# Reordering the time-mix projections of a two-layer block: k first, the low-rank products of decay and a between its passes

## The reference, cut to what matters

```python
xr, xw, xk, xv, xa, xg = (h + hh * mu[i] for i in range(6))
r = xr @ w_r
w = -jax.nn.softplus(-(w0 + jnp.tanh(xw @ w1) @ w2)) - 0.5   # w1: 1024 x 64
k = xk @ w_k
v = xv @ w_v
a = jax.nn.sigmoid(a0 + (xa @ a1) @ a2)                      # a1: 1024 x 64
g = jax.nn.sigmoid(xg @ g1) @ g2                             # g1: 1024 x 160
kk = (k * k_k) / head_norm(k * k_k)
k = k * (1.0 + (a - 1.0) * k_a)
decay = jnp.exp(-jnp.exp(w))
```

## Time and profile before

| | |
|---|---|
| median of three runs | 2342.24 us (2339.76 to 2344.61) |
| the profiled execution, its own time | 2346.41 us |
| its span, first to last instruction | 2344.3 us |
| PE busy (weight loads) | 2075.5 us, 89% (1585.3 us) |
| DVE, ACT, POOL busy | 838.8, 803.3, 687.1 us |
| mean granted TensorE clock | 0.927 |
| first matmul of a projection; last of v | 35.7; 294.2 us |

### The profile page before, as it was taken

The page is one execution under the profiler, slowest core; times in us unless marked ns, Lnnn a source line. Parts: engine busy times, 40 slices in busy tenths (PEclk is TensorE's granted clock), DMA queues, the critical chain, the costliest instruction groups (busy, mean ns, idle before and its releaser), DMA issues.

```text
span 2344.3 us, 36168 instructions
## 1 busy us (share of the span) xinstructions
PE 2075.5 (89%) x15556; PEld 1585.3 (68%) x15556; DVE 838.8 (36%) x1217; ACT 803.3 (34%) x1043; POOL 687.1 (29%) x198
## 2 busy tenths in 40 slices
PE   5979876667999999988997789999998999979997
PEld 2656856653778888866665467888887885747764
DVE  4876153333332221023656633222101234252333
ACT  5663332233244432132124434443212413232232
POOL 0333232201233344423310023334443423203430
PEclk7689999996799999999998789999999998889999
DMA  3112100001123332222210012333322211112110
GB/s 110 36 54 67 41 4 4 4 23 46 54 72 93 104 89 99 99 80 73 68 41 18 1 55 72 95 102 89 99 99 90 90 55 54 36 59 90 54 54 36
DMA packets 190702, 147.06 MB, mean 63 GB/s; under 512 B 6888, under 2 KB 188351, under 8 KB 190576
## 3 DMA queue, kind: packets, MB, share of 16 engines
q1 hardware_dynamic: 190576, 145.18, 20.1%
HBM read 143.06 MB, written 2.10 MB: 62 GB/s over the span
## 4 chain that ended last, share of the span: by engine, by line
PE 77%; DVE 9%; ACT 6%; issue 4%; POOL 2%; DMA 1%; SPq 0%; DVEq 0%; ACTq 0%
PE psum L2227 20%; PE psum L2229 19%; PE psum L2228 19%; PE psum L2376 4%; DVE X_lo L1610 2%; ACT w_hi L1110 1%; PE psum L2303 1%; POOL w_lo L989 1%; DVE xf L1740 1%; PE psum L2233 1%; PE psum L2638 1%; ACT xf L1142 1%; DVE col L2002 1%; PE psum L2601 1%; PE psum L2795 1%
## 5 line engine op out<-in xcount | busy, mean ns | idle before, releaser
L989 POOL TENSOR_TENSOR w_lo<-weight_raw,w_hi 128x2048 fp32r<-128x2048 f32 (+2 forms) x136 | 605.3, 4452 | 1433.3 <-ACT w_hi L1110 1433.1
L2227 PE MATMUL psum<-X_hi,w_hi 128*128 128x512 f32 x1544 | 644.2, 417 | 62.1 <-DVE X_lo L1610 42.5
L2229 PE MATMUL psum<-X_hi,w_lo 128*128 128x512 f32 x1544 | 617.4, 400 | 0.0
L2228 PE MATMUL psum<-X_lo,w_hi 128*128 128x512 f32 x1544 | 617.3, 400 | 0.0
L2227 PEld LDWEIGHTS psum<-X_hi,w_hi 128*128 128x128 f32 x1544 | 299.5, 194 | 181.5 <-issue 95.8
L1110 ACT ACTIVATE w_hi<-weight_raw 128x2048 fp32r<-128x2048 f32 (+2 forms) x136 | 251.7, 1850 | 381.2 <-PE psum L2229 369.8
L2228 PEld LDWEIGHTS psum<-X_lo,w_hi 128*128 128x128 f32 x1544 | 300.2, 194 | 64.6 <-issue 6.7
L2229 PEld LDWEIGHTS psum<-X_hi,w_lo 128*128 128x128 f32 x1544 | 299.3, 194 | 65.9
L1659 DVE TENSOR_TENSOR sgate<-rt,psum 128x512 f32<-128x512 f32 x44 | 30.2, 687 | 320.4 <-PE psum L2229 320.4
L2227 PE MATMUL psum<-hb_hi,w_hi 128*128 128x512 f32 x352 | 136.9, 389 | 0.0
L2228 PE MATMUL psum<-hb_lo,w_hi 128*128 128x512 f32 x352 | 136.9, 389 | 0.0
(11 more groups left out here) (426 smaller groups left out, 2639.2 us busy)
## 6 DMA issues: line engine op xcount, KB each, us to landing
weight_raw<-in_ffn_w_gu SPq DMA_DIRECT2D x88, 512.0 KB, 4.9
weight_raw<-in_l_w_in SPq DMA_DIRECT2D x45, 512.0 KB, 4.6
weight_raw<-in_ffn_w_down SPq DMA_DIRECT2D x40, 512.0 KB, 3.7
weight_raw<-in_kv_w SPq DMA_DIRECT2D x16, 512.0 KB, 4.1
weight_raw<-in_l_w_out SPq DMA_DIRECT2D x16, 512.0 KB, 4.1
weight_raw<-in_rw_w_k SPq DMA_DIRECT2D x8, 512.0 KB, 4.1
weight_raw<-in_rw_w_r SPq DMA_DIRECT2D x8, 512.0 KB, 4.0
weight_raw<-in_rw_w_v SPq DMA_DIRECT2D x8, 512.0 KB, 4.5
```

The lines of the kernel that those rows point to most:

```text
L989: ins = pool.tensor_tensor(l, r, h.bitcast(F32), ALU.subtract)
L2227: pe.matmul(ps, wh, xh, start=start, stop=False, skip_group_check=True)
L2228: pe.matmul(ps, wh, xl, start=False, stop=False, skip_group_check=True)
L2229: return pe.matmul(ps, wl, xh, start=False, stop=stop, skip_group_check=True)
```

## The change

The plan's products a1, w1, a2, w2 are taken out. The low-rank products become jobs on PSUM banks 4 to 7 that stand inside the passes of k. Their inputs go through a ring of three tiles (`ring_f`, `ring_hi`, `ring_lo`) instead of X_hi and X_lo, and their weights have buffers of their own, which are loaded behind the parameter rows.

```diff
-    for n in ("a1", "w1", "a2", "w2", "k", "r", "g1", "v"):
+    for n in ("k", "r", "g1", "v"):
         j.step(n)
+    j.add(("first", 0), 4, "A")
+    j.add(("first", 1), 5, "A")
+    for m in range(2 * KT):
+        j.add(("second", m), 6 + m % 2, "A")
+LORA_AT = {9 + j: j for j in range(2 * KT)}
+SECOND_AT = {25: (0, 1), 26: (2, 3), 27: (4, 5), 28: (6, 7), 29: (8, 9), 30: (10, 11, 12), 31: (13, 14, 15)}
+RING = 3
+HEAD_SUM_AT = {("r", 0, 5): 0, ("r", 1, 0): 1, ("r", 1, 3): 2, ("r", 1, 7): 3, ("r", 2, 2): 4, ("r", 2, 5): 5,
+               ("r", 3, 1): 6, ("r", 3, 4): 7}
+HEAD_INV_AT = {("v", 0, 2): 0, ("v", 0, 4): 1, ("v", 0, 6): 2, ("v", 1, 0): 3, ("v", 1, 2): 4, ("v", 1, 4): 5,
+               ("v", 1, 6): 6, ("v", 2, 0): 7}
```

A slot number here is 8 x pass + tile of k (0 to 31): first-stage product j stands ahead of tile 9 + j, the second-stage ones ahead of tiles 25 to 31. On POOL:

```diff
+            low(0)
+            low(1)
+            for i, (r, h, l) in enumerate(((first_raw[:, :, :], first_hi[:, :, :], first_lo[:, :, :]),
+                                           (second_raw[:, :], second_hi[:, :], second_lo[:, :]))):
+                pool.wait_ge(lora_hi, i + 1)
+                pool.tensor_tensor(l, r, h.bitcast(F32), ALU.subtract).then_inc(lora_lo, 1)
+            for n in range(2, 5):
+                low(n)
+            for k in range(4):
+                before(k)
+            low(5)
+            for k in range(4, KT):
+                before(k)
+            low(6)
+            low(7)
```

On ACT (ring_high(j) first issues ring_first(j + 1), then waits for ring_mixed of j and for PE's use of j - 3):

```diff
             high(0)
+            high(1)
...
+            lora_high(0)
+            mix_high(0, MU_K)
+            lora_high(1)
+            ring_first(0)
+            keys_out(0)
+            high(2)
+            for j in range(7):
+                ring_high(j)
+            keys_out(1)
+            high(3)
+            for j in range(7, 15):
+                ring_high(j)
+                if j == 10:
+                    low_rank(0, ACT.Tanh)
+            keys_out(2)
+            high(4)
+            ring_high(15)
+            low_rank(1, ACT.Copy)
+            mix_high(1, MU_R, lambda k: sigmoids(25 + k))
+            keys_out(3)
+            wait_step(act, PL.first["k"] + 3)
             for i in range(4):
+                high(5 + i)
+                for k in (2 * i, 2 * i + 1):
+                    if k >= 2:
+                        act.wait_ge(sq_k_used, k - 1)
+                    key_tile(k)
+            mix_high(2, MU_G)
...
             next_slot(s)
+            mix_high(3, MU_V)
```

On DVE:

```diff
+            split(0, mixed(0, MU_K))
+            for j in range(2 * KT):
+                f, mu = ring_f[j % RING], 8 * (MU_W, MU_A)[j // KT] + j % KT
+                dve.wait_ge(ring_half, j + 1)
+                dve.scalar_tensor_tensor(out=f[:, :], in0=h_sb[:, j % KT, 0:S], scalar=pcol("rw_mu", mu), in1=f[:, :],
+                                         op0=ALU.mult, op1=ALU.add).then_inc(ring_mixed, 1)
+                if j:
+                    ring_low(j - 1)
+                if j == 12:
+                    mid_low(1, halves(0))
+            ring_low(2 * KT - 1)
+            split(1, mixed_r)
+            for k in range(2, KT):
+                decay(k)
+            for k in range(3):
+                keys(k)
+            receptance(0)
+            for k in range(3, 6):
+                keys(k)
+            receptance(1)
+            keys(6)
+            keys(7)
+            receptance(2)
+            split(2, mixed(2, MU_G))
...
+            receptance(3)
+            split(3, mixed(3, MU_V))
+            for k in range(KT):
+                key_norm(k)
```

More of the change, by code:

```diff
@@ L838, in hn_pe_count, with wait_ring_used @@
             return at - NORM_AT.index(at) + k + 1
+        def wait_ring_used(eng, j):
+            if j % KT == KT - 1:
+                wait_done(eng, ("first", j // KT))
+            else:
+                eng.wait_ge(ring_used, j - j // KT + 1)
         block = ctx.enter_context(nc.Block())
@@ L1250, in sigmoids, with keys_out @@
+            def sigmoids(slot):
+                for m in SECOND_AT.get(slot, ()):
+                    key, k = ("second", m), m % KT
+                    wait_done(act, key)
+                    act.activation((u0, af)[m // KT][:, k, :], bank(job_banks(key)[0]), ACT.Sigmoid,
+                                   bias=pcol(("rw_w0", "rw_a0")[m // KT], k)).then_inc(job_a, 1)
+            def keys_out(i):
+                s = PL.first["k"] + i
                 act.wait_ge(kstep, step_end(s))
                 for m in range(2):
-                    last = act.activation(dst[:, 2 * i + m, 0:S], bank(step_banks(s)[m]), ACT.Sigmoid,
-                                          bias=pcol(vec, 2 * i + m))
+                    last = act.activation(kf[:, 2 * i + m, :], bank(step_banks(s)[m]), ACT.Copy)
@@ L2362, in _, with low_rank, part @@
-            for name in ("k", "r"):
-                for i in range(4):
-                    features(PL.first[name] + i, XV["x" + name] if i == 0 else None, parts=beside(name, i))
+            def low_rank(i):
+                def part(k):
+                    slot = 8 * i + k
+                    if slot in LORA_AT:
+                        j = LORA_AT[slot]
+                        n, at = j // KT, j % KT
+                        b = job_banks(("first", n))[0]
+                        if at == 0:
+                            wait_banks(pe, ("first", n))
+                            pe.wait_ge(lora_lo, 1)
+                        elif at == KT - 1:
+                            order[0] += 1
+                        pe.wait_ge(ring_xl, j + 1)
+                        three(bank(b), (first_hi[:, at, :], first_lo[:, at, :]),
+                              (ring_hi[:, j % RING, :], ring_lo[:, j % RING, :]), at == 0, at == KT - 1
+                              ).then_inc(ring_used if at < KT - 1 else job_done, 1)
+                    for m in SECOND_AT.get(slot, ()):
+                        n, c = m // KT, slice(P * (m % KT), P * (m % KT) + P)
+                        rows = halves(n)
+                        pe.wait_ge(lora_lo, 2)
+                        pe.wait_ge(mid_l, n + 1)
+                        b = begin(("second", m))
+                        three(bank(b), (second_hi[rows, c], second_lo[rows, c]), (mid_hi[rows, :], mid_lo[rows, :]),
+                              True, True).then_inc(job_done, 1)
+                return part
@@ L2365, in _ @@
+            for i in range(4):
+                features(PL.first["k"] + i, XV["xk"] if i == 0 else None, parts=low_rank(i))
+            for i in range(4):
+                features(PL.first["r"] + i, XV["xr"] if i == 0 else None, parts=beside("r", i))
             features(PL.first["g1"], XV["xg"], cols=(slice(0, 128), slice(32, 160)))
-            product("v", XV["xv"], tokens)
+            for i in range(4):
+                tokens(PL.first["v"] + i, XV["xv"] if i == 0 else None, parts=beside("v", i))
```

193 lines of the change are left out of this document (73 added, 120 removed).

## The result

The kernel after has a median of 2355.29 us and the kernel before, run beside it, one of 2344.43 us (18 executions each). The ratio is 1.0045, with a 95% interval of 1.0032 to 1.0058: slower by 10.5 us (7.5 to 13.6). The forecast was +10.8. One execution of the kernel after took 2987.75 us at a mean clock of 0.638; it is a slow one and not in the ratio, as all ratios here are of fast runs.

A forecast was written before the change was run, and what follows sets the result against it. PE's chain ended last for 77% of the span, and up to 80 us of PE looked free. The terms summed to +10.8 us at v's end, which on the median of 2342.2 gave 2353 us, range 2328 to 2367.

The forecast's parts named there:

- Start: Ahead of k: POOL's two full slots and first-stage weights hold DVE's operations on h, done 10.5 us later, at 43.9.
- First pass: k's first pass: first X_lo at 46.0, last 14.4 us later, pass ends at 61.8 with PE at 2.4 GHz.
- Seams: Between k's passes: ACT's eviction and copy, POOL's slot and ring work cost 8.9 us, plus 2.5 for PE's clock.
- Pass ends: k's second to fourth pass end at 87.6, 115.3 and 149.5; in the fourth PE needs 2.73 us a tile.
- From k's end to the gate's mixing: During r: DVE's operations and POOL's subtractions taking turns sum to 61.3 us, so the gate's mixing starts at 210.8.
- Gate, norm, v: Gate's last X_lo at 227.1; unhidden inverse norm and v's slot take 12.6 us; v's second pass at 263.8.
- v's end: End of v's passes: 305.0, against 294.2 before, a sum of +10.8 us.
- three passes, 36.8: v's last three passes: 36.8 us from the earlier profile, plus five spreading jobs of 0.9 us, 4.4 together.
- Rival 1: POOL's subtractions miss DVE's work, so PE's gaps fill: -28.6 us, 2314; chance 0.15 with its partial forms.
- Rival 2: Balance even: PE returns to 2.4 GHz at once, POOL meets DVE somewhat less often; 2338 to 2346; chance 0.18.
- Rival 3: PE stays at 1.2 GHz in k's passes: 2392; chance 0.07.
- Rival 4: Products move but nothing else does: PE runs in order, so a late ring tile holds k; within the forecast.

The follow-up runs named there:

- e2: The changed kernel with POOL's subtraction of slots 2, 3 and 4 waiting until DVE has made the first ring tiles behind each seam; 2341.27 us, ratio 0.9996.
- e1: The changed kernel with ACT's ring copies moved ahead of the seams, three ring tiles before the first eviction of k; 2343.17 us, ratio 0.9991.
- e5: The changed kernel with receptance(0) put behind the first key tile and receptance(1) behind the fourth, earlier on DVE; 2356.74 us, ratio 1.0043.
- e6: The changed kernel with v's weight slot and mixing ahead of the keys' inverse norm, its spreading moved to v's second to fourth pass; 2351.22 us, ratio 1.0026.
- e9: e1 with POOL's slots 2, 3, 4 held until three ring tiles are in store, first-stage weights until k's mixing is done; 2337.92 us, ratio 0.9965.
- e4: The changed kernel with POOL's subtractions of slots 0 to 7 and the low-rank weights replaced by memsets that read nothing; 2327.91 us, ratio 0.9928.
- e3: The changed kernel with POOL's second weight slot and first-stage weights held until k's eight X_lo are done; 2349.59 us, ratio 1.0016.
- e8: e9, e5 and e6 together: ring ahead, POOL's subtractions placed, receptances early, norm behind v's mixing; 2331.47 us, ratio 0.9942.

## Why the prediction was right

By its own steps:

- **Start.** "h is done at 43.9, 10.5 us later": 42.25, 8.9 later. The first matmul is at 44.57 instead of 46.0. POOL had its slot at 25.1, not 27.2, since the rows landed no later. What POOL blocked was not h, whose operations ran undisturbed, but three small operations ahead of it. Two of these have only one input, and "both operands in SBUF" did not cover them. The trace of before had such a row already, beside a slot of POOL from 174.78 to 179.34: a one-input maximum on 16x512, which the sum put at 0.3 us and which takes 0.41 in after, with POOL idle.

```profile
176.64 2.98 DVE L1810 TENSOR_SCALAR sgf<-sgf 16x512 f32<-16x512 f32 x1 [2.02 <-ACT sgf L1305]
```

- **First pass.** Predicted end 61.8; its first eviction starts at 61.20. PE is at the high level over most of it (clock 0.90), and waits 0.6 us at four of its tiles for DVE's X_lo, so that the mixing sets its length, as assumed.
- **Seams.** Idle times of 7.5, 8.8 (8.9 less 0.1) and 8.2 against 7.43, 8.79 and 8.19. e2 shows which part is POOL's (3.7 to 3.9), and e1 that the rest is ACT's order. The 2.5 us a seam for the clock is no constant: PE was at 1.2 GHz for 10.2, 6.8 and 10.2 us around the three, and busy for 5.1, 3.1 and 4.0 of them. Half of that lost is 6.1 us by estimate, where the sum had 7.5.
- **Pass ends.** 87.6, 115.3 and 149.5 against 87.1, 114.1 and 151.5. The last is late by the fourth pass alone, which took 29.2 us and not 26.0. The term that was too small is "PE 2.73" for a tile: with its second-stage products a tile took 3.17. PE is busy for 28.83 of the 29.20 us. At each change between products of 64 and of 128 rows two matmuls start 0.32 to 0.34 us after the one ahead instead of 0.23; why, no run shows. Over seven such tiles that is some 3 us, by estimate.

```profile
134.37 0.50 PE L2296 MATMUL psum<-X_hi,w_hi 128*128 128x512 f32 x1
...
137.54 0.50 PE L2296 MATMUL psum<-X_hi,w_hi 128*128 128x512 f32 x1
```

- **From k's end to the gate's mixing.** 61.3 against 59.2, and the mechanism as it stood: six scans take 14.33 us, with small subtractions and one slot of POOL (5.53 us from 157.85) in turns between them, and two operations of `keys` are held for 5.06 and 5.11. e5 shows that DVE's sum sets it. PE's waits "ended by DVE's receptance or ACT's Square" are all there, 5.12, 0.52 and 2.07 us. The sum gave each of POOL's slots its full length. The gate's, 2.93 us from 200.13, began beside a receptance and held DVE's next operation to 2.32 us instead of 0.75, so that some 1.3 of its 2.9 us cost nothing.
- **Gate, norm, v.** Last gate X_lo 227.1 against 226.9; v's last X_lo 255.3 against 255.0; v's second pass 263.8 against 263.5. The gap ahead of v is 11.78 us. e6 shows that the norm's own part in it was 6.2.
- **v's end.** 305.0 against 302.4, the largest error. The step that failed is "three passes, 36.8": that row of before contained 4.6 us at a clock of 0.51, which stood in the earlier trace rows beside it, and I carried it over as if it were the passes' price. After, the same passes with five jobs take 38.8 and not 41.2 us, at a clock of 1.00. In e5 and e9, whose low stretch does lie on the second pass, they take 41.3 and 41.2. So the term hangs on where that stretch falls, which the sum had no step for.

```profile
241.06 0.55 PE L2296 MATMUL psum<-w_hi,X_hi 128*128 128x256 f32 x1 [11.78 <-DVE X_lo L1670]
...
152.30 14.33 DVE L1848 TENSOR_TENSOR_SCAN rf<-keep,u 128x512 f32<-128x512 f32 x6
...
171.56 5.06 DVE L1818 TENSOR_TENSOR af<-af,grow 128x512 f32<-128x512 f32 x1
...
201.29 2.32 DVE L1812 SCALAR_TENSOR_TENSOR u<-kf,pv,u 128x512 f32<-128x512 f32 x1 [0.64 <-ACT u L1328]
```

These are the gap ahead of v on PE, and DVE's scans, an operation of `keys` held up by a slot, and the one beside the gate's. The sum was +10.8 us at v's end; measured are +8.1 in the profile and +10.5 in the ratio. That the ratio comes within 0.3 us is in part luck: single steps were off by 1.4 us (start), 2.0 (k's end, the other way), 2.1 (k's end to the gate) and 2.4 (v's passes). The rule that I drew on (the Trainium skill, SBUF — State Buffer, "Who interferes with whom", its practical consequences) agrees with the rows shown here, the 4.48 us of the ring's mix beside a subtraction among them. The page says more than I took from it, though. Besides the two-input case against a GpSimd instruction that reads SBUF, it says that VectorE in a two-port performance mode contends with GpSimd. The rows of e4 fit both halves: beside memsets the two-input `lamp` is free (0.28 us), and the one-input `oka` is held to the end of one (1.81 instead of 0.17). That `oka` runs in such a mode is inferred; no trace names it.

**The rivals.** Rival 1 (the gaps are filled) fell with POOL's reads in place, and e4 shows that even without them it would have been 2328. Its step that was too bold is k at 125.7, where e4's k ended at 135.3. The 125.7 had 2.5 us a seam for the clock in it. Of the 9.6 us 5.5 lie in the fourth pass, which took 31.5 us and not 26.0: its tiles cost more than 2.73 there too, and PE was at 1.2 GHz for the first 9.2 us of it. Rival 2 had PE back at 2.4 GHz at once behind each gap, and it wasn't. Without the 6.1 us estimated above v would have ended near 296, 2 us after before; no run tests that. Rival 3 (1.2 GHz all through k) didn't occur: PE came up to 2.4 GHz in each pass. Rival 4 (a late ring tile holds k as well) is what happened at each seam: in the second one PE is busy for 0.11 of 8.90 us. As it says itself, it lay within the forecast.

What stays open: how many us the low stretches of PE cost in the median of many executions. The profiles of e3, e4, e5, e6, e8 and e9 have a stretch at 1.2 GHz at the start of v's second pass, those of after, e1 and e2 don't, and in e3, e4, e5 and e9 it moved v's end by 2.4 to 3.0 us. One profile each can't say whether that belongs to the edit. So differences of 3 us or less between two positions of v's end in the table say nothing of the edits.

## What to carry to other kernels

Ahead of filling gaps on TensorE, list what VectorE and GpSimd do in them: a GpSimd subtraction that reads SBUF (4.5 us here) holds up the gap by nearly its full length if the next VectorE operation is what the gap waits for. Placed behind that operation by one semaphore wait, it gave back 3.7 to 3.9 us of each gap here. In a kernel whose engines take their instructions in order, a job put between two passes waits for all that stands ahead of its producers too (here ACT's eviction and slot copy, 3 us), so its producers must be issued ahead of these, and the ring must hold more than that time. And take a pass's price from a stretch in which the granted clock is 1.00, with the low stretches as a term of their own.

## What the runs showed of the hardware that I had not expected

- A VectorE operation with one SBUF input on 128 x 8 elements was held for 4.40 us by a GpSimd subtraction (0.17 us alone, in e3), and for 1.81 us by a GpSimd memset (e4).
- Where VectorE and GpSimd both had a row of work, they took turns operation by operation: the six scans of 1.48 us each (8.90 / 6 in e4, small subtractions beside them there too) took 2.39 beside the subtractions and a whole slot.
- The clock behind a gap is not a fixed price. In one execution of after PE was at 1.2 GHz for 10.2 us (from 64.8), 6.8 us (from 92.1) and 10.2 us (from 116.0) at gaps of 7.43, 8.79 and 8.19 us. From 116.0 to 126.2 it was idle for the first six, and then ran at the low level for four more (columns as in the stretches above):

```profile
116.00:126.20 10.20, 3.88 (x9) 2.81 (x9) 4.70 (x2) 3.74 (x6) 4.50 (x1) 0.51 0.31 103
```

- Where a low stretch falls matters as much as its length. In after 6.8 us of it (256.0 to 262.8) lay on the end of v's first pass, where the second had to wait for its weight slot anyway, and cost next to nothing: the first pass takes 22.5 us from first matmul to the second pass's, as in e5, which is at 1.00 there from 246 on. In e3, e4, e5 and e9 as much of it began with the second pass or just ahead of it, and v's last three passes took 41.8, 41.8, 41.3 and 41.2 us instead of 38.8.
